# First tiles of three output projections begun inside the attention ahead of them

## The chip, the cores and the metric

The kernel runs on one core of one Trainium2 chip, in one launch. The metric is the device time of an execution in microseconds (us). Engines: TensorE (PE, with its weight loads PEld), VectorE (DVE), ScalarE (ACT), GpSimd (POOL) and SyncE (SP, which only issues transfers here). Lower is better.

## The reference

A decoder of two layers takes 1024 prompt tokens and 8 sample tokens (one per sequence of a batch of 8), width 1024, all in fp32. In words and cut to what matters:

```python
for l in range(2):
    hp = rms_norm(xp, norm_mix[l])
    # layer 0: short convolution beside banded attention; layer 1: pooling beside dilated attention
    mix = concat(conv_or_pool(hp), windowed_attention(hp))
    xp = xp + mix @ w_out
    mk, mv = rms_norm(mem, norm_mem[l]) @ w_ca_kv[l]
    q = rms_norm(xp, norm_ca[l]) @ w_ca_q[l]
    xp = xp + softmax(q @ mk.T / 16) @ mv @ w_ca_o[l]      # 4 heads of 256, 256 memory rows
    g, u = rms_norm(xp, norm_ffn[l]) @ w_ffn_in[l]
    xp = xp + (silu(g) * u) @ w_ffn_out[l]
y = rms_norm(xp, norm_final)
```

The same is done for the sample tokens, with their own caches, and new rows of the caches are outputs too. Layer 1's attention is dilated: three patterns of keys, combined by their softmax weights.

## The kernel before, in words

Activations lie transposed: partitions are features, a tensor `[128, 8, 1032]` is 8 chunks of 128 features by 1032 tokens. A linear map runs in units: one unit is one block of 128 output features, made of 8 chunks. The tokens are cut in three tiles of 344 columns, so a unit is 3 tiles x 8 chunks. To keep fp32's precision each operand is split in a high part (`*_hi`, type fp32r) and a low part (`*_lo`, the rest), and a chunk takes three matmuls: high x high, high x low and low x high. So one tile is 24 matmuls and one unit 72. They are issued by `passes` (line 712), called by `unit`.

Weights come by SP into `w_raw`, two slots; GpSimd makes their high part (line 563) and low part (line 567), half a unit at a time, into the slot of `w_hi` and `w_lo` that frees up; it may do so for the next unit once the present one has started (`unit_started`).

Attention writes its result into `mix1` (layer 1's pooling and dilated attention) or `mixc` (cross attention). Before the output projection that result is split too: `split` on ScalarE copies it into `h_hi` or `g_hi` (`copy`, line 1306), and `split` on VectorE subtracts into `h_lo` or `g_lo` (line 1906), in twelve pieces: three tiles by four groups of two chunks. Tensor for tensor:

- `out1` (from `linear_out`, 4 turns of 2 units) multiplies `h_hi`, `h_lo`; its results go to banks 0 to 2 of `linear`, and VectorE adds each into `x` (line 1924), squares are summed for the next norm (line 1876).
- `caout0` and `caout1` (from `ca_out`) do the same with `g_hi`, `g_lo`; here VectorE adds at line 2105, and beside this starts to make sums of `x` for the feed-forward part (`combine`, tiles named `c`).

What sets the order around this is written out by hand, engine by engine, with semaphores. Cross attention (`cross`) runs four heads. Each has units for queries and keys, then nine jobs: "S" scores (line 780), "T" turning the probabilities (line 816), "V" mixing the values (line 852), and at the end "R", the turning of the sample's result (line 823). Scores alternate between `ps_scores` and bank 0 of `linear`. In heads 0 to 2 the last steps are interleaved with the first key unit of the next head (`next_key`, line 956); in the last head `next_key` returns at once. The dilated attention of layer 1 runs in four pairs of heads; a pair's jobs ("S" line 1170, "T" line 1194, "V" lines 1224 and 1233) stand in the tables `DIL_KEY`, `DIL_FILL` and `DIL_DRAIN` between the tiles of the linear units. For the last pair there are none left, so its jobs follow each other. VectorE computes the maxima (line 2594), ScalarE the exponentials (line 1766) and the copies of turned blocks (line 1306, `pt`), VectorE the scaled results (lines 2632, 2634).

## Time and profile before

| | |
|---|---|
| median of 3 runs | 3014.34 us (3012.35 to 3015.76) |
| the profiled execution | 3013.3 us |
| its span, first to last instruction | 3011.5 us |
| mean granted TensorE clock | 0.986 |
| busy: PE, DVE, POOL, ACT | 96%, 55%, 45%, 26% |

The span is the time of the trace; the 1.8 us between it and the execution's own time lie around it. Starts in the rows are us from the span's start. The granted clock is a share of full speed, 2.4 GHz; 0.5 is 1.2 GHz. A matmul's row shows how long it took from start to finish; they overlap, so the pace is read from starts. In square brackets stands the idle time of the engine before a row, and what ended it.

### The profile page before, as it was taken

How to read it: one execution, taken by the hardware profiler on the slowest of the kernel's cores; microseconds unless marked ns; L12 is line 12 of the kernel's file. 1: busy time of each engine (PE TensorE's matmuls, PEld its weight loads, DVE VectorE, ACT ScalarE, POOL GpSimd, SP SyncE). 2: the span in 40 equal slices, each digit the busy share in tenths (PEclk: the TensorE clock that was granted, in tenths of full speed). 3: DMA queues.
4: the chain of work that ended last, by engine and by line, in shares of the span. 5: the costliest groups of instructions: out<-in, count | busy, mean ns of one | idle time of the engine just before them, and what ended most of it. 6: DMA issues, size and time to landing. Idle time of an engine off the chain costs nothing.

```text
span 3011.5 us, 58301 instructions
## 1 busy us (share of the span) xinstructions
PE 2877.5 (96%) x21217; PEld 2735.5 (91%) x21217; DVE 1642.7 (55%) x3290; ACT 796.9 (26%) x1832; POOL 1344.6 (45%) x1156
## 2 busy tenths in 40 slices
PE   7999999999899999999999999999997999999997
PEld 6888998989899999999887778988897999999996
DVE  5555642248755555655943336522368565565655
ACT  3333322132212221112323334212223111221112
POOL 2222343424665666655331102433336665565664
PEclk9999999999999999999999999999998999999998
DMA  3011133421111111111122221243210111111112
GB/s 129 29 35 35 52 122 113 151 74 35 43 48 49 49 50 49 54 42 56 60 71 78 78 71 64 85 145 121 106 42 30 55 56 42 56 42 56 54 44 71
DMA packets 52534, 198.83 MB, mean 66 GB/s; under 512 B 6961, under 2 KB 14001, under 8 KB 49081
## 3 DMA queue, kind: packets, MB, share of 16 engines
q1 hardware_dynamic: 36912, 130.51, 13.6%
q10 hardware_dynamic: 15504, 66.71, 6.2%
q8 instruction: 79, 1.29, 0.2%
q14 instruction: 39, 0.31, 0.0%
HBM read 184.34 MB, written 13.10 MB: 66 GB/s over the span
## 4 chain that ended last, share of the span: by engine, by line
PE 86%; DVE 7%; issue 3%; ACT 3%; POOL 1%; DMA 0%; ACTq 0%; DVEq 0%; POOLq 0%; SPq 0%
PE linear L712 46%; PE ps_scores L997 11%; PE ps_turned L997 8%; PE ps_mixed L997 4%; PE linear L997 4%; PE ps_mixed L852 2%; PE ps_turned L816 1%; PE ps_turned L1194 1%; PE ps_scores L780 1%; PE ps_mixed L1224 1%; PE ps_scores L1170 1%; DVE g_lo L1906 1%; POOL w_lo L567 1%; PE linear L780 1%; PE ps_mixed L848 1%
## 5 line engine op out<-in xcount | busy, mean ns | idle before, releaser
L567 POOL TENSOR_TENSOR w_lo<-w_raw,w_hi 128x512 fp32r<-128x512 f32 x492 | 687.7, 1407 | 259.1 <-ACT w_hi L1306 234.0
L563 POOL TENSOR_SCALAR w_hi<-w_raw 128x512 fp32r<-128x512 f32 x324 | 215.4, 678 | 1176.2 <-PE linear L712 993.1
L712 PE MATMUL linear<-h_hi,w_hi 128*128 128x344 f32 x1152 | 384.1, 333 | 27.9 <-POOL w_lo L567 13.3
L712 PE MATMUL linear<-h_lo,w_hi 128*128 128x344 f32 x1152 | 371.9, 323 | 0.0
L712 PE MATMUL linear<-h_hi,w_lo 128*128 128x344 f32 x1152 | 371.7, 323 | 0.0
L712 PE MATMUL linear<-hid_hi,w_hi 128*128 128x344 f32 x1056 | 339.1, 321 | 5.3 <-DVE x L2345 4.2
L712 PE MATMUL linear<-hid_hi,w_lo 128*128 128x344 f32 x1056 | 339.3, 321 | 0.0
L712 PE MATMUL linear<-hid_lo,w_hi 128*128 128x344 f32 x1056 | 338.9, 321 | 0.0
L2304 DVE TENSOR_TENSOR x<-linear,x 128x344 f32<-128x344 f32 x480 | 246.7, 514 | 144.4 <-PE linear L712 142.0
L997 PE MATMUL ps_scores<-c,w_hi 128*128 128x258 f32 x1584 | 304.6, 284 | 7.9 <-DVE c L2093 7.9
L712 PEld LDWEIGHTS linear<-h_hi,w_hi 128*128 128x128 f32 x1152 | 220.0, 191 | 45.6 <-issue 36.7
L712 PE MATMUL linear<-g_hi,w_hi 128*128 128x344 f32 x768 | 250.0, 326 | 5.8 <-DVE g_lo L1906 4.9
L997 PEld LDWEIGHTS ps_scores<-c,w_hi 128*128 128x128 f32 x1584 | 246.9, 190 | 8.6 <-DVE c L2093 8.3
L712 PE MATMUL linear<-g_hi,w_lo 128*128 128x344 f32 x768 | 246.6, 321 | 0.0
L712 PE MATMUL linear<-g_lo,w_hi 128*128 128x344 f32 x768 | 246.6, 321 | 0.0
L997 PE MATMUL ps_turned<-c,w_hi 128*128 128x258 f32 x1232 | 232.2, 285 | 10.9 <-ACT rs L1313 10.9
L1306 ACT ACTIVATE w_hi<-w_raw 128x512 fp32r<-128x512 f32 x168 | 100.8, 624 | 486.9 <-PE ps_mixed L997 295.8
L997 PE MATMUL ps_scores<-c,w_lo 128*128 128x258 f32 x792 | 225.3, 285 | 0.0
L567 POOL TENSOR_TENSOR w_lo<-w_sum,w_hi 128x512 fp32r<-128x512 f32 x132 | 178.2, 1350 | 96.2 <-ACT w_hi L1306 95.7
L712 PEld LDWEIGHTS linear<-h_lo,w_hi 128*128 128x128 f32 x1152 | 220.2, 191 | 0.5 <-issue 0.2
L712 PEld LDWEIGHTS linear<-h_hi,w_lo 128*128 128x128 f32 x1152 | 219.8, 191 | 0.0
L712 PEld LDWEIGHTS linear<-hid_hi,w_hi 128*128 128x128 f32 x1056 | 198.8, 188 | 6.5 <-DVE x L2345 5.0
(354 smaller groups left out, 6483.4 us busy)
## 6 DMA issues: line engine op xcount, KB each, us to landing
w_raw<-in_w SPq DMA_DIRECT2D x246, 512.0 KB, 3.5
kv_slotc<-in_mem_cache_k ACTq DMA_DIRECT2D x8, 2048.0 KB, 8.2
kv_slotc<-in_mem_cache_v ACTq DMA_DIRECT2D x8, 2048.0 KB, 10.2
kv_slot<-in_dil_k ACTq DMA_DIRECT2D x4, 1536.0 KB, 6.4
kv_slot<-in_dil_v ACTq DMA_DIRECT2D x4, 1536.0 KB, 6.6
out_y<-answer ACTq DMA_DIRECT2D x6, 688.0 KB, 6.7
x<-in_x ACTq DMA_DIRECT2D x2, 1376.0 KB, 10.2
out_dil_v_out<-v ACTq DMA_DIRECT2D x4, 516.0 KB, 3.6
```

Of the source, the lines that this page charges most:

```text
L563: pool.tensor_scalar(out, src, 1.0, 0.0, ALU.mult, ALU.add).then_inc(sem["hi_split"], 1)
L567: return pool.tensor_tensor(out, src, hi.bitcast(F32), ALU.subtract).then_inc(sem[event], 1)
L712: mm = pe.matmul(out, w[:, slot, cols], a, start=(k == 0 and j == 0), stop=(k == n - 1 and j == 2))
L780: mm = pe.matmul(sc[:, 0:MEM], q[:, c, P * job:P * job + P], k[:, c, :], start=(c == 0), stop=(c == 1))
L816: mm = pe.transpose(ps_t[:, o:o + P], p[job % RING[kind]][:, o:o + P], ident[:])
L848: mm = pe.matmul(o, w, a, start=(j < 4), stop=(j >= len(todo) - 4), skip_group_check=True)
L852: mm = pe.matmul(ps_o[:, P * c:P * c + P], vnat[:, m, P * c:P * c + P], pt[:, P * m:P * m + P], start=(m == 0), stop=(m == 1))
L997: mm = pe.matmul(lin[bank][:, 0:PART], w[:, b % 4 // 2, c], a, start=(b in OPENING and kp == 0 and j == 0), stop=(kp == CH // 2 - 1 and j ...
L1170: mm = pe.matmul(ps_s[:, 512 * h:512 * h + P * nb], q1[r:r + HEAD, P * qb:P * qb + P], k1[r:r + HEAD, P * kb:P * kb + P * nb], start=True, ...
L1194: mm = pe.transpose(ps_t[:, to:to + P], p1[i][k % 3][:, 512 * h + P * b:512 * h + P * b + P], ident[:])
L1306: return act.activation(out, in_, ACT.Copy, **kw)
L2304: dve.tensor_tensor(x[:, 4 * half + n, a:b], lin[tile_plan(ph)[p][0]][:, 0:TILE], x[:, 4 * half + n, a:b], ALU.add).then_inc(sem["freed_dv ...
```

## The change

Nine of the twelve pieces of the split are called `SOONER` (three tiles by the chunk groups 0 to 2, that is chunks 0 to 5), the other three `LATER` (chunks 6 and 7). In the last dilated pair, and in the last cross attention head of each layer, ScalarE and VectorE make the `SOONER` pieces between the attention's own instructions. A new function `begin` issues matmuls of the first unit's tiles there: in the dilated pair chunks 0 to 5 of all three tiles, two chunks after each of eight score jobs and two behind `DIL_DRAIN`'s first entry; in each last head chunks 0 to 5 of tile 0, in four places (2, 2, 1, 1 chunks). Behind the attention the `LATER` pieces are split and `unit` adds chunks 6 and 7 to the tiles begun. The loops over turns of these projections are written out on TensorE, `p1_late` lies at the end of `h_lo`, and layer 0's `out0` keeps its twelve pieces. Line numbers in the order rows are those of the file that they come from.

```diff
     raise KeyError(phase)
+SOONER = [(t, q) for t in range(3) for q in range(3)]
+LATER = [(t, 3) for t in range(3)]
@@ -238,7 +242,8 @@
...
-        return at("lo_ready", source, 0, 4 * t + k // 2 + 1) if k % 2 == 0 else None
+        pieces = [(t_, q) for t_ in range(3) for q in range(4)] if source == "split0" else SOONER + LATER
+        return at("lo_ready", source, 0, pieces.index((t, k // 2)) + 1) if k % 2 == 0 else None
@@ -437,7 +442,7 @@
...
-        p1_late = over_h(("p1_late", [P, 1024], F32))[0]
+        p1_late = over(("p1_late", [P, 1024], F32), start=h_place + 4 * TOK * (2 * CH - 1))[0]
@@ -714,7 +721,26 @@
...
+            def begin(phase, t, chunks, hi, lo, slot):
+                a, b = TILES[t]
+                ready = chunk_ready({"out1": "split1"}.get(phase, f"casplit{phase[-1]}"))
+                if chunks[0] == 0:
+                    pe.wait_ge(sem["half_split"], at("half_split", phase, 0, 1))
+                    pe.wait_ge(sem["freed_dve"], bank_wait(phase, 0, t)[1])
+                for k in chunks:
+                    if t == 0 and k == CH // 2:
+                        pe.wait_ge(sem["unit_split"], at("unit_split", phase, 0, 1))
+                    if ready(t, k) is not None:
+                        pe.wait_ge(sem["lo_ready"], ready(t, k))
+                    c = slice(P * k, P * k + P)
+                    for j, (w, x_) in enumerate(((w_hi, hi), (w_hi, lo), (w_lo, hi))):
+                        mm = pe.matmul(lin[t][:, 0:b - a], w[:, slot, c], x_[:, k, a:b], start=(k == 0 and j == 0), stop=False)
+                        if t == 0 and k == 0 and j == 0:
+                            mm.then_inc(sem["unit_started"], 1)
@@ -722,12 +748,13 @@
...
-                    pe.wait_ge(sem[name], value)
+                    if t not in begun:
+                        pe.wait_ge(sem[name], value)
...
+                           pause=pause and (lambda: pause(t)), begun=6 if t in begun else 0)
@@ -870,6 +897,13 @@
...
+                if phase == "out1":
+                    p = unit(phase, 0, 0, 0, TILES, hi, lo, chunk_ready(source), begun=(0, 1, 2))
+                    unit(phase, 0, 1, p, TILES, hi, lo)
+                    for i in range(1, 4):
+                        for u in range(2):
+                            unit(phase, i, u, 3 * u, TILES, hi, lo)
+                    return
@@ -879,11 +913,11 @@
...
                 ph, source = f"caout{l}", f"casplit{l}"
-                enter(ph)
-                with pe.Fori(0, 3) as i:
-                    p = 0
+                p = unit(ph, 0, 0, 0, TILES, g_hi, g_lo, chunk_ready(source), begun=(0,))
+                unit(ph, 0, 1, p, TILES, g_hi, g_lo)
+                for i in range(1, 3):
                     for u in range(2):
-                        p = unit(ph, i, u, p, TILES, g_hi, g_lo, chunk_ready(source) if u == 0 else None)
+                        unit(ph, i, u, 3 * u, TILES, g_hi, g_lo)
@@ -945,6 +979,9 @@
                     def next_key(part):
                         if h == CA_HEADS - 1:
+                            if part == 0:
+                                pe.wait_ge(sem["exped"], at("exped", ph, 0, order_s("mem", 6) + 1))
+                            begin(f"caout{l}", 0, ((0, 1), (2, 3), (4,), (5,))[part], g_hi, g_lo, 0)
@@ -1275,6 +1312,13 @@
                     for what, k in DIL_FILL.get(position, ()):
                         step(what, k)
+                        if i == PAIRS - 1 and what == "S" and k in range(4, 12):
+                            begin_out(k - 4)
+                def begin_out(n):
+                    t, q = SOONER[n]
+                    begin("out1", t, (2 * q, 2 * q + 1), h_hi, h_lo, 0)
@@ -1290,6 +1334,8 @@
                 last = step
             for position in range(5):
                 drain(position)
+                if position == 0:
+                    begin_out(8)
@@ -1335,16 +1381,19 @@
...
-            def split(phase, mix, before, hi):
+            def high_piece(mix, hi, t, q):
+                c, (a, b) = slice(2 * q, 2 * q + 2), TILES[t]
+                copy(hi[:, c, a:b], mix[:, c, a:b]).then_inc(sem["hi_ready"], 1)
+            def split(phase, mix, hi, pieces):
                 act.wait_ge(sem["mixed_out"], at("mixed_out", phase))
                 act.wait_ge(sem["freed_dve"], at("freed_dve", phase))
                 act.wait_ge(sem["tile_done"], at("tile_done", phase))
-                for t, (a, b) in enumerate(TILES):
-                    for q in range(4):
-                        c = slice(2 * q, 2 * q + 2)
-                        copy(hi[:, c, a:b], mix[:, c, a:b]).then_inc(sem["hi_ready"], 1)
+                for piece in pieces:
+                    high_piece(mix, hi, *piece)
@@ -1474,11 +1523,24 @@
...
+                        sooner(7)
+                    def sooner(n):
+                        if h == CA_HEADS - 1:
+                            past_waits()
+                            high_piece(mixc, g_hi, *SOONER[n])
+                    if h == CA_HEADS - 1:
+                        act.wait_ge(sem["tile_done"], at("tile_done", ph, 0, 7))
+                        for n in range(4):
+                            sooner(n)
                     attention(ph, 0, "mem", mixc, 2 * h, p_c, ptc, psc, drawnc[h], values=(kv_slotc[:, :], dram["mem_cache_v"][l, h]),
-                              ahead={("T", 0): values_turned, ("V", 4): values_stored}, redrawn=False)
+                              ahead={("T", 0): values_turned, ("V", 1): lambda: sooner(4), ("V", 2): lambda: sooner(5),
+                                     ("V", 3): lambda: sooner(6), ("V", 4): values_stored, ("V", 5): lambda: sooner(8)}, redrawn=False)
                 redraw(CA_HEADS - 1)
-                split(f"casplit{l}", mixc, ph, g_hi)
+                split(f"casplit{l}", mixc, g_hi, LATER)
@@ -1770,6 +1832,10 @@
...
+                    if i == PAIRS - 1 and what == "S" and k in range(1, 10):
+                        act.wait_ge(sem["tile_done"], at("tile_done", ph, 0, 6))
+                        high_piece(mix1, h_hi, *SOONER[k - 1])
                     if what == "S":
                         if SCORE_ORDER.index(k):
                             exponential(SCORE_ORDER[SCORE_ORDER.index(k) - 1])
@@ -1897,14 +1963,13 @@
...
+            def split(phase, mix, hi, lo, pieces, done=0):
+                for n, (t, q) in enumerate(pieces):
+                    c, (a, b) = slice(2 * q, 2 * q + 2), TILES[t]
+                    dve.wait_ge(sem["hi_ready"], at("hi_ready", phase, 0, done + n + 1))
+                    dve.tensor_tensor(lo[:, c, a:b], mix[:, c, a:b], hi[:, c, a:b].bitcast(F32), ALU.subtract
+                                      ).then_inc(sem["lo_ready"], 1)
@@ -2044,18 +2109,28 @@
...
+                    def sooner(n):
+                        past_waits()
+                        split(f"casplit{l}", mixc, g_hi, g_lo, SOONER[n:n + 1], n)
...
                     for done, job in zip(jobs, jobs[1:]):
                         if job == 2:
                             empty(ph, 0, 8, vc[h][:, 1, :], mem_rs[:], MEM)
                         bias_of(job)
                         normalise(done)
+                        if h == CA_HEADS - 1:
+                            sooner(jobs.index(done))
                     normalise(jobs[-1])
+                    if h == CA_HEADS - 1:
+                        sooner(8)
...
-                split(f"casplit{l}", mixc, g_hi, g_lo)
+                split(f"casplit{l}", mixc, g_hi, g_lo, LATER, 9)
@@ -2637,6 +2712,9 @@
                     if what == "S":
                         peaks(k)
+                        if i == PAIRS - 1 and k in range(2, 11):
+                            past_waits()
+                            split("split1", mix1, h_hi, h_lo, SOONER[k - 2:k - 1], k - 2)
```

TensorE, layer 0's last head, after the last score job (`kc`, `qc`). Before:

```order
L780 MATMUL ps_scores<-kc,qc 128x256 x2
L852 MATMUL ps_mixed<-ptc,vnatc 128x128 x4
L816 MATMUL ps_turned<-ident,pc_ring 128x128 x2
L852 MATMUL ps_mixed<-ptc,vnatc 128x128 x4
L816 MATMUL ps_turned<-ident,pc_ring 128x128 x2
L852 MATMUL ps_mixed<-ptc,vnatc 128x128 x4
L809 MATMUL ps_turned<-ident,psc 128x128 x2
```

and in the changed kernel:

```order
L807 MATMUL ps_scores<-kc,qc 128x256 x2
L879 MATMUL ps_mixed<-ptc,vnatc 128x128 x4
L843 MATMUL ps_turned<-ident,pc_ring 128x128 x2
L739 MATMUL linear<-g_hi,w_hi 128x344
L739 MATMUL linear<-g_lo,w_hi 128x344
L739 MATMUL linear<-g_hi,w_lo 128x344
L739 MATMUL linear<-g_hi,w_hi 128x344
L739 MATMUL linear<-g_lo,w_hi 128x344
L739 MATMUL linear<-g_hi,w_lo 128x344
L879 MATMUL ps_mixed<-ptc,vnatc 128x128 x4
L843 MATMUL ps_turned<-ident,pc_ring 128x128 x2
```

Six multiplies of `caout0`'s first tile stand between a turning and the mixing behind it.

VectorE, last dilated pair, from the end of job 2's maxima on (`p_late`; the ISA rows are the maxima with their masks). Before:

```order
L2594 ISA p_late,peak_104<-ps_scores,mask_102 128x512
L2594 ISA peak_104 128x1
L2594 ISA p_ring,peak_104<-ps_scores,mask_102,peak_104 128x384
L2594 ISA peak_104 128x1
L2594 ISA p_ring,peak_104<-ps_scores,mask_102,peak_104 128x384
L2594 ISA peak_104 128x1
L2605 TENSOR_SCALAR binv_106<-peak_104 128x2
L2622 TENSOR_TENSOR den_105<-den_105 128x2
L2625 RECIPROCAL binv_106<-den_105 128x2
```

and in the changed kernel:

```order
L2669 ISA p_late,peak_104<-ps_scores,mask_102 128x512
L2669 ISA peak_104 128x1
L1971 TENSOR_TENSOR h_lo<-mix_90,h_hi 128x2x344
L2669 ISA p_ring,peak_104<-ps_scores,mask_102,peak_104 128x384
L2669 ISA peak_104 128x1
L2669 ISA p_ring,peak_104<-ps_scores,mask_102,peak_104 128x384
L2669 ISA peak_104 128x1
L2680 TENSOR_SCALAR binv_106<-peak_104 128x2
L1971 TENSOR_TENSOR h_lo<-mix_90,h_hi 128x2x344
L2697 TENSOR_TENSOR den_105<-den_105 128x2
L2700 RECIPROCAL binv_106<-den_105 128x2
```

A low part stands behind each pair of maxima, and the sums and reciprocal (`den`, `binv`) on which the mixing waits have moved behind it.

ScalarE, start of the same pair. Before:

```order
L1827 DMA out_dil_k_out<-k_92 128x1032
L1766 ACTIVATE p_ring,den_105<-p_ring,binv_106 128x512 x4
L1306 ACTIVATE pt_98<-ps_turned 128x512 x2
L1766 ACTIVATE p_late,den_105<-p_late,binv_106 128x512 x2
L1306 ACTIVATE pt_98<-ps_turned 128x512 x2
```

and in the changed kernel:

```order
L1893 DMA out_dil_k_out<-k_92 128x1032
L1352 ACTIVATE h_hi<-mix_90 128x2x344
L1828 ACTIVATE p_ring,den_105<-p_ring,binv_106 128x512 x2
L1352 ACTIVATE h_hi<-mix_90 128x2x344
L1828 ACTIVATE p_ring,den_105<-p_ring,binv_106 128x512 x2
L1352 ACTIVATE pt_98<-ps_turned 128x512 x2
L1352 ACTIVATE h_hi<-mix_90 128x2x344
```

A high part stands ahead of each exponential; two of them have moved in front of the copy `pt`.

## Rows read from the trace of the kernel before

**Rows 1.** The page's part 1: engine, busy us, share, instructions.

```profile
PE 2877.5 (96%) x21217; PEld 2735.5 (91%) x21217; DVE 1642.7 (55%) x3290; ACT 796.9 (26%) x1832; POOL 1344.6 (45%) x1156
```

**Rows 2.** Chain of waits, 640 to 730 us: start, us, what ran.

```profile
641.48 12.53 DVE g_lo L1906 x12
...
656.57 64.45 PE linear L712 x408
```

**Rows 3.** Timeline, TensorE, layer 0's last head: start, us, operation, [idle before].

```profile
630.56 0.38 PE L816 MATMUL ps_turned<-ident,pc_ring 128*128 128x128 f32 x2
631.56 1.16 PE L852 MATMUL ps_mixed<-ptc,vnatc 128*128 128x128 f32 x8 [0.61 <-ACT ptc L1306]
...
639.66 0.60 PE L823 MATMUL ps_turned<-ident,drawn_last 128*128 128x128 f32 x4
642.50 0.40 PE L712 MATMUL linear<-g_hi,w_hi 128*128 128x344 f32 x1 [2.24 <-DVE g_lo L1906]
```

**Rows 4.** The same view, third head.

```profile
572.94 0.38 PE L816 MATMUL ps_turned<-ident,pc_ring 128*128 128x128 f32 x2
573.08 0.36 PE L956 MATMUL linear<-mem_hi,w_hi 128*128 128x256 f32 x1
...
573.94 1.16 PE L852 MATMUL ps_mixed<-ptc,vnatc 128*128 128x128 f32 x8
```

**Rows 5.** Windows: us, busy us (instructions) by engine, granted clock, DMA share, GB/s.

```profile
643.50:647.00 3.50, 3.50 (x15) 3.50 (x14) 3.50 (x4) 3.50 (x6) 3.50 (x3) 0.51 0.00 0
1836.68:1840.00 3.32, 3.32 (x12) 3.32 (x13) 3.32 (x4) 3.32 (x6) 2.49 (x3) 0.50 0.55 229
```

**Rows 6.** Low parts, line 1906, then high parts: count, ns min/median/max, first and last start.

```profile
L1906 DVE TENSOR_TENSOR g_lo<-mixc,g_hi x24: 862/868/1961, 641.5 to 2179.1; 128x688 fp32r<-128x688 f32 x24
...
L1306 ACT ACTIVATE g_hi<-mixc x24: 757/762/776, 640.7 to 2174.0; 128x688 fp32r<-128x688 f32 x24
```

**Rows 7.** Timeline, layer 0's last head: VectorE, then ScalarE.

```profile
625.84 0.42 DVE L1951 TENSOR_REDUCE peak<-ps_scores 128x1 f32<-128x256 f32 x1 [0.93 <-PE ps_scores L780]
...
627.84 0.42 DVE L1951 TENSOR_REDUCE peak<-linear 128x1 f32<-128x256 f32 x1 [0.93 <-PE linear L780]
...
624.85 0.38 ACT L1306 ACTIVATE mixc<-ps_mixed 128x256 f32<-128x256 f32 x1 [0.89 <-PE ps_mixed L852]
```

**Rows 8.** Timeline, GpSimd: layer 1's last head, then the start of `out1`.

```profile
2141.88 1.28 POOL L563 TENSOR_SCALAR w_hi<-w_raw 128x512 fp32r<-128x512 f32 x2 [3.47 <-PE linear L712]
2143.12 2.52 POOL L567 TENSOR_TENSOR w_lo<-w_raw,w_hi 128x512 fp32r<-128x512 f32 x2
...
1837.51 2.28 POOL L563 TENSOR_SCALAR w_hi<-w_raw 128x512 fp32r<-128x512 f32 x2 [57.41 <-PE linear L712]
```

**Rows 9.** Waits of TensorE, 1798 to 1828.5 us: us in total, times, longest.

```profile
PE ps_turned L1194 <- ACT pt L1306: 2.2, 5, 0.7
PE ps_scores L1170 <- DVE peak L2594: 1.4, 3, 0.7
```

**Rows 10.** Windows, the last dilated pair from its fourth job on.

```profile
1797.94:1828.82 30.88, 26.64 (x289) 18.04 (x288) 15.95 (x73) 21.43 (x60) 0.00 (x0) 1.00 0.16 53
```

**Rows 11.** Timeline, ScalarE, start of the last dilated pair.

```profile
1795.52 0.71 ACT L1766 ACTIVATE p_ring<-p_ring,binv 128x512 f32<-128x512 f32 x1
1796.14 0.19 ACT L1766 ACTIVATION_READ_ACCUMULATOR p_ring<-p_ring,binv 128x1 f32 x1
1796.23 1.06 ACT L1306 ACTIVATE pt<-ps_turned 128x512 f32<-128x512 f32 x2
```

**Rows 12.** Chain of waits at the start of `out1`, then TensorE's timeline there.

```profile
1836.68 13.35 PE linear L712 x69
...
1833.45 0.44 PE L1249 MATMUL ps_turned<-ident,drawn 128*128 128x128 f32 x2 [0.50 <-ACT drawn L1306]
1836.68 0.63 PE L712 MATMUL linear<-h_hi,w_hi 128*128 128x344 f32 x1 [2.80 <-DVE h_lo L1906]
```

**Rows 13.** Waits of VectorE, 656.57 to 721 us; then a window behind `caout`.

```profile
DVE x L2105 <- PE linear L712: 15.1, 12, 2.0
...
735.00:750.00 15.00, 9.94 (x60) 8.93 (x59) 14.72 (x17) 3.11 (x6) 11.38 (x9) 0.89 0.12 36
```

More of the change, by code:

```diff
@@ L697, in enter, with passes @@
                 pe.wait_ge(sem["freed_dve"], at("freed_dve", phase))
-            def passes(out, slot, terms, unit_first=False, ready=None, second_half=None, pause=None):
+            def passes(out, slot, terms, unit_first=False, ready=None, second_half=None, pause=None, begun=0):
                 n = len(terms)
                 for k, (cols, hi, lo) in enumerate(terms):
+                    if k < begun:
+                        continue
                     if pause and k == n // 2:
@@ L715, in passes, with unit @@
                 mm.then_inc(sem["tile_done"], 1)
-            def unit(phase, turn, u, p, tiles, hi, lo, ready=None, after=None, slot=None, pause=None):
+            def begin(phase, t, chunks, hi, lo, slot):
[14 more added lines that the diff above has]
+                            mm.then_inc(sem["unit_started"], 1)
+            def unit(phase, turn, u, p, tiles, hi, lo, ready=None, after=None, slot=None, pause=None, begun=()):
                 pe.wait_ge(sem["half_split"], at("half_split", phase, turn, u + 1))
@@ L729, in unit @@
                            second_half=at("unit_split", phase, turn, u + 1) if t == 0 else None,
-                           pause=pause and (lambda: pause(t)))
+                           pause=pause and (lambda: pause(t)), begun=6 if t in begun else 0)
                     if after:
@@ L1695, in out_and_memory @@
                 act.dma_start(mem_raw[:], dram["mem"]).then_inc(loads[f"mem{l}"], 16)
-                split(f"split{l}", mix, f"att{l}", h_hi)
+                split(f"split{l}", mix, h_hi, LATER if l else [(t, q) for t in range(3) for q in range(4)])
                 act.wait_ge(loads[f"mem{l}"], 16)
@@ L1898, in inverse @@
                     inverse_tile(name, t)
-            def split(phase, mix, hi, lo):
-                for t, (a, b) in enumerate(TILES):
-                    for q in range(4):
-                        c = slice(2 * q, 2 * q + 2)
-                        dve.wait_ge(sem["hi_ready"], at("hi_ready", phase, 0, 4 * t + q + 1))
-                        dve.tensor_tensor(lo[:, c, a:b], mix[:, c, a:b], hi[:, c, a:b].bitcast(F32), ALU.subtract
-                                          ).then_inc(sem["lo_ready"], 1)
+            def split(phase, mix, hi, lo, pieces, done=0):
[4 more added lines that the diff above has]
+                                      ).then_inc(sem["lo_ready"], 1)
             def empty(phase, turn, p, out, factor, w=TILE):
@@ L2489, in out_and_memory @@
                 dve.wait_ge(sem["mixed_out"], at("mixed_out", f"split{l}"))
-                split(f"split{l}", mix, h_hi, h_lo)
+                split(f"split{l}", mix, h_hi, h_lo, LATER if l else [(t, q) for t in range(3) for q in range(4)], 9 * l)
                 zero(ph)
```

## The prediction

> **What bounds the kernel now.** I read the page's busy shares first: the reader is to see TensorE busy for 96% of the span and nothing else near it [rows 1]. So a change gains only where it removes time in which TensorE has nothing to run, or runs slowly. The views to read next are the chain of waits and the timelines around the three joints that the diff touches: last head of cross attention to `caout` in layer 0 (near 642 us), the same in layer 1 (near 2168 us, with the same pattern), and last dilated pair to `out1` (near 1837 us). A multiply of 344 columns takes 0.158 us at full clock when they follow each other (64.45 us for 408) [rows 2].
>
> At the first joint the last turning of the attention ends at about 640.3, and `caout` starts at 642.50 after 2.24 us of idle, released by VectorE's first `g_lo` [rows 3]. VectorE then works without a break on twelve low parts (12.53 us from 641.48), and another 2.56 us pass until TensorE starts the second unit at 656.57 [rows 2]. So the first unit, 72 multiplies or 11.38 us of work, takes 14.07 us. Of the 2.7 us of excess the clock makes 1.7: from 643.5 to 647.0 it was granted 0.51, and 0.49 x 3.5 us is lost [rows 5]. The other 1.0 us is waiting for low parts and for the bank that VectorE empties late.
>
> At the dilated joint the idle stretch is 2.80 us, and then the clock is at the lower of its two levels, 1.2 GHz [rows 5, 12]. The first unit takes the 13.35 us of 69 multiplies plus 3 x 0.158, 13.82 us [rows 12].
>
> **The change at the two cross attention joints.** High and low parts of nine of the twelve pieces (a piece is two chunks by one tile) are made earlier, during the last head. 18 multiplies of tile 0 go to four places between the attention's last steps; behind it three pieces are made as before and 54 of the first unit's 72 multiplies remain. The wait is not removed: the last piece of tile 0 still goes copy, ScalarE high part, VectorE low part, so the 2.24 us stand [rows 3].
>
> From the first multiply behind the attention to the second unit's it will take 54 x 0.158 = 8.53 us plus the same 1.7 us of slow clock, 10.2 us in place of 14.07: 3.9 us less. VectorE is no limit there: it has three low parts in place of twelve, and the 2.56 us behind them [rows 2], so it is free after some 5 us where TensorE needs 10.
>
> What is added. The third head already carries six multiplies of 256 columns between these same steps, and its steps are as far apart as the last head's: 572.94 to 573.94 there, 630.56 to 631.56 here, both 1.00 us [rows 3, 4]. So they are hidden. Six of 344 columns are longer by 6 x 0.158 x 88 / 344 = 0.24 us, some 0.2 behind the pipeline's start; two of the places get six, the other two three, which fit: 0.4 us in all. ScalarE's pieces take 0.76 us [rows 6]; four go before the head's first exponential, five into idle stretches such as the 0.89 us before the row at 624.85 [rows 7]: nothing. Without that idle each would cost its 0.76. VectorE's pieces take 0.87 us where nothing disturbs them and up to 1.96 us beside GpSimd's splits of weights [rows 6]. VectorE idles 0.93 us in each job of 2.0 us [rows 7], so 0.87 fits by a hair. The early ones meet GpSimd's 2.5 us of low parts (at 2143.12 in layer 1 [rows 8]), and a multiply of attention waits for what stands behind them: I put 0.5 us, between nothing and the 1.09 us by which a disturbed piece is longer. Sum for one joint: 3.9 - 0.4 - 0.5 = 3.0 us; both 6.0 us.
>
> Two edits cost nothing. The loops over turns are written out: the 64.45 us of multiplies [rows 2] run over three turns' ends without a gap, so the loop cost nothing either. `p1_late` moves from the start of `h_hi` to the last chunk of `h_lo`, which no early piece writes.
>
> Is the gain kept? From 735 us VectorE is busy 14.72 of 15 us and TensorE waits for it [rows 13]: a place where a gain could end. But up to 721 VectorE itself waited 15.1 us in twelve places for TensorE's tiles [rows 13], so its load begins when the tiles come, and moves with them. I keep all of it.
>
> **The change at the dilated joint.** Here all nine early pieces get their multiplies inside the pair: 54, or 8.53 us, in nine groups of 0.95 us; 18 close the first unit. Behind the attention stand 8.53 us less, with the wait of 2.80 us and the slow clock unchanged, because the last three pieces are still begun behind the attention's last copy. The price is the pair's own length. From its fourth job on TensorE waits only 2.2 + 1.4 = 3.6 us [rows 9]; if the groups filled all of it, the pair would be 8.53 - 3.6 = 4.9 us longer. That is the lower bound. To it I add one high part of 0.76 us [rows 6] that lands where ScalarE has no idle at all, before the copy at 1796.23, which follows its exponentials at once [rows 11]; and one disturbed low part. GpSimd splits the next unit's weights as soon as the first group starts, so this moves from 1837.51 [rows 8] into the pair, and 1.96 - 0.87 = 1.1 us [rows 6] goes on VectorE. 4.9 + 0.8 + 1.1 = 6.8 us longer, a gain of 8.53 - 6.8 = 1.7 us. The upper bound is everything on the path: 8.5 of TensorE, 9 x 0.76 = 6.8 of ScalarE and 9 x 0.87 = 7.8 of VectorE, 23.1 us longer. I stay near the lower one since ScalarE is busy 21.4 and VectorE 16.0 of 30.9 us [rows 10]: both have room, though ScalarE comes to 28.2.
>
> The trace has low parts of 0.87 us and of 1.96 us [rows 6], and GpSimd's high parts took 2.28 us beside them, 1.28 otherwise [rows 8]. The Trainium skill, "SBUF — State Buffer", section "Who interferes with whom", says that a VectorE instruction with two SBUF inputs and a GpSimd one that reads SBUF take a port pair as an exclusive lock, and that the second blocks until the first is done. By that rule all four GpSimd instructions that move, 1.28 + 2.52 = 3.8 us undisturbed [rows 8], could hold up VectorE inside the pair; it would be 4.9 + 0.8 + 3.8 = 9.5 us longer and this joint a loss of 1.0. That speaks against the change, on the side of the third rival below.
>
> **Sum.** 6.0 + 1.7 = 7.7 us. The profiled execution took 3013.3 us, span 3011.5 and 1.8 around it; less 7.7 that is 3005.6. It lies 1.0 us under the median of the runs (3014.34), so I predict 3006.6 us. A measurement can tell about 0.2%, 6.0 us, from no change: below 3008.3 is faster, above 3020.4 slower.
>
> **Rivals.** First, the clock holds. With the attention's idle places filled, TensorE is not granted the lower level at these joints, and the losses go: 1.7 + 1.7 and, at the dilated joint, 13.82 - 11.38 = 2.4 us, together 5.8: 3000.8. For it: more is fed before each joint. Against it: the idle stretches of 2.24 and 2.80 us remain, and the clock was low behind both kinds [rows 5, 12]. The Trainium skill, "TensorE: Matmul & The Clock Gate", section "What's actually happening", says that activity releases the throttle and that idle is the throttled state. The low clock behind the gaps agrees, and by that rule a fuller attention could keep it up. Chance 0.14.
>
> Second, the gain at the cross joints is not kept: VectorE's full stretch from 735 us does not move, and only the dilated 1.7 us stay: 3012.6. The 15.1 us of waits speak against it. Chance 0.08.
>
> Third, the dilated pair gives a loss: its steps form one chain through three engines, each of which gets pieces, and it becomes 10.5 us longer, 2.0 more than it gives: 6.0 - 2.0 = 4.0 gained, 3010.3. ScalarE's 28.2 of 30.9 us speaks for it, the idle of VectorE against [rows 10]. Chance 0.16.
>
> Fourth, slower: in the same chain nearly every piece stands in series, 23.1 us longer, 14.6 more than the 8.5 given; less the 6.0 that is 8.6 us slower: 3022.9. From 14.5 us of lengthening on, the kernel is slower than before. Against it: ScalarE idles 9.5 and VectorE 14.9 us of those 30.9 [rows 10], and pieces have nothing to wait for when an engine idles. Chance 0.03.
>
> The forecast has 0.59; its own range, 3003 to 3009.5, comes from 2.4 to 3.9 us for each cross joint and 0 to 3.6 at the dilated one. Some 0.12 of it lies beyond 3008.3. Faster: 0.47 + 0.14 and 0.03 of the third rival where it is milder, 0.64; slower 0.03; same 0.33. The range of 8 in 10 is 3000.5 to 3012.5.
>
> **What would show it.** In the profile after: the idle before the first multiply behind each attention still 2.2 and 2.8 us; from it to the second unit about 10 us at the cross joints, with no wait for VectorE's sums; the dilated pair 6 to 8 us longer from its second score job to the last turning, with hardly any wait for ScalarE; low parts of 0.87 us there but for one to four long ones; GpSimd's split of the second unit inside the attention. Wrong would be: a pair 10 us longer (third rival), full clock behind the joints (first), or TensorE waiting 3 us longer for VectorE after 735 us (second).

## The result and the profile after

The changed kernel takes 2997.15 us (median of 5 runs, 2994.33 to 2997.83) where the kernel before takes 3014.34 (3012.35 to 3018.01 in 5 runs): ratio 0.9941, 95% interval 0.9928 to 0.9955. It is faster by 17.2 us, or 0.6%, where 7.7 us were forecast and the far end of the range was 13.8. The profiled execution took 2994.33, its span 2992.5.

The page's part 1, beside [rows 1]:

```profile
PE 2870.5 (96%) x21217; PEld 2729.6 (91%) x21217; DVE 1638.3 (55%) x3290; ACT 795.9 (27%) x1832; POOL 1338.4 (45%) x1156
```

The instructions are the same in number, and TensorE is busy for 7.0 us less; this row does not tell why. The other 12 us of the 19.0 by which the span is shorter are idle time that went.

The chain at layer 0's joint, then at layer 1's, beside [rows 2]:

```profile
641.20 0.89 DVE g_lo L1971
642.23 74.45 PE linear L719 x462
...
2155.78 72.91 PE linear L719 x462
```

VectorE has one low part on the chain in place of twelve, and TensorE runs through. Less the 64.45 us of the 408 behind it, the 54 multiplies of the first unit take 10.0 us in layer 0 and 8.5 in layer 1, in place of 14.07. Two windows tell these apart (us, busy us by engine, granted clock):

```profile
642.80:646.10 3.30, 3.30 (x13) 3.30 (x13) 3.01 (x6) 0.00 (x0) 0.00 (x0) 0.50 0.00 0
...
2156.00:2164.00 8.00, 8.00 (x52) 8.00 (x52) 4.87 (x9) 0.99 (x3) 0.00 (x0) 1.00 0.01 2
```

TensorE in the last head of layer 0, beside [rows 3]:

```profile
630.17 0.38 PE L843 MATMUL ps_turned<-ident,pc_ring 128*128 128x128 f32 x2
630.31 0.41 PE L739 MATMUL linear<-g_hi,w_hi 128*128 128x344 f32 x1
...
631.34 1.05 PE L879 MATMUL ps_mixed<-ptc,vnatc 128*128 128x128 f32 x8
...
639.39 0.60 PE L850 MATMUL ps_turned<-ident,drawn_last 128*128 128x128 f32 x4
642.23 0.39 PE L719 MATMUL linear<-g_hi,w_hi 128*128 128x344 f32 x1 [2.24 <-DVE g_lo L1971]
```

The six multiplies fit (1.17 us from turning to mixing, 1.00 before), and the 2.24 us of idle stand. Low parts, beside [rows 6], and then GpSimd's split of `out1`'s second unit, now inside the pair, beside [rows 8]:

```profile
L1971 DVE TENSOR_TENSOR h_lo<-mix,h_hi x24: 859/875/1966, 308.9 to 1833.2; 128x688 fp32r<-128x688 f32 x24
L1971 DVE TENSOR_TENSOR g_lo<-mixc,g_hi x24: 865/868/1955, 614.4 to 2156.3; 128x688 fp32r<-128x688 f32 x24
```

```profile
1791.22 1.20 POOL L568 TENSOR_SCALAR w_hi<-w_raw 128x512 fp32r<-128x512 f32 x2 [21.33 <-PE linear L739]
1792.39 3.13 POOL L572 TENSOR_TENSOR w_lo<-w_raw,w_hi 128x512 fp32r<-128x512 f32 x2
```

The longest low part in the pair took 1.05 us. TensorE's waits, 1785 to 1827 us, beside [rows 9]:

```profile
PE ps_mixed L1248 <- ACT pt L1352: 0.8, 1, 0.8
PE ps_mixed L1261 <- DVE mix L2709: 0.7, 1, 0.7
PE ps_turned L1231 <- ACT pt L1352: 0.2, 1, 0.2
```

Only the last row lies in the stretch that [rows 9] covers (1788.5 to 1824.4 us here): 3.6 us in the kernel before, 0.2 now. The other two stand behind it in both kernels, with 0.72 and 0.79 us.

Windows of the pair from the same multiply to the same multiply as in [rows 10], and of the joint behind it, beside [rows 5]:

```profile
1788.51:1824.77 36.26, 35.35 (x344) 26.78 (x343) 22.75 (x81) 25.32 (x66) 4.30 (x4) 1.00 0.18 60
...
1834.10:1837.30 3.20, 3.20 (x13) 3.20 (x12) 2.21 (x5) 0.96 (x2) 0.00 (x0) 0.50 0.09 36
```

From its fourth job on the pair is 5.4 us longer (36.26 against 30.88). TensorE's first multiply behind it and the chain from there, beside [rows 12]: the 2.80 us of idle stand here too, and the stretch at the low clock is 3.4 us long where it was 6.8.

```profile
1832.64 0.40 PE L719 MATMUL linear<-h_hi,w_hi 128*128 128x344 f32 x1 [2.80 <-DVE h_lo L1971]
```

```profile
1832.64 83.95 PE linear L719 x522
```

**A ledger of the two traces.** All of VectorE's instructions but the low parts come in the same order in every kernel here, so any two traces can be laid side by side at them. In each stretch between the same two instructions, the changed kernel's time less that of the kernel before is: layer 0's last head and joint -3.5 us (0.5 longer, then 4.0 shorter); last dilated pair +6.15, its joint -9.2, so -3.1; layer 1's head and joint -5.0. Together 11.6. The other 7.4 us lie in stretches whose instructions are the same: the first 47 us -0.8, layer 0's feed-forward turns -1.9, the norms from 1440 to 1530 us -3.8, the start of layer 1's feed-forward part -1.3, the end +0.5, all else -0.1. So there were two questions: why the joints give more than 7.7, and whether the 7.4 is chance.

### The profile page after: what moved, and what is told of

It reads as the page before. It is cut to its first block, busy times and chain, and to the rows that moved or that the text cites. A ratio compares the mean times of both kernels' runs of the same rounds, so it can differ in the third digit from the quotient of the medians.

```text
span 2992.5 us, 58217 instructions
## 1 busy us (share of the span) xinstructions
PE 2870.5 (96%) x21217; PEld 2729.6 (91%) x21217; DVE 1638.3 (55%) x3290; ACT 795.9 (27%) x1832; POOL 1338.4 (45%) x1156
## 4 chain that ended last, share of the span: by engine, by line
PE 89%; DVE 6%; issue 2%; ACT 2%; POOL 0%; DMA 0%; ACTq 0%; DVEq 0%; POOLq 0%; SPq 0%
PE linear L719 47%; PE ps_scores L1034 12%; PE ps_turned L1034 8%; PE ps_mixed L1034 4%; PE linear L1034 4%; PE ps_mixed L879 2%; PE ps_turned L843 1%; PE ps_turned L1231 1%; PE ps_scores L1207 1%; PE ps_mixed L1261 1%; PE ps_scores L807 1%; PE linear L807 1%; PE ps_mixed L875 1%; PE ps_mixed L887 1%; PE linear L993 1%
## 5 line engine op out<-in xcount | busy, mean ns | idle before, releaser
L568 POOL TENSOR_SCALAR w_hi<-w_raw 128x512 fp32r<-128x512 f32 x324 | 209.1, 658 | 1164.0 <-PE linear L719 937.6
L719 PE MATMUL linear<-h_hi,w_hi 128*128 128x344 f32 x1134 | 376.4, 332 | 27.5 <-POOL w_lo L572 13.1
L719 PE MATMUL linear<-h_lo,w_hi 128*128 128x344 f32 x1134 | 364.8, 322 | 0.0
L719 PE MATMUL linear<-h_hi,w_lo 128*128 128x344 f32 x1134 | 364.7, 322 | 0.0
```

Source lines behind the costliest of these rows:

```text
L568: pool.tensor_scalar(out, src, 1.0, 0.0, ALU.mult, ALU.add).then_inc(sem["hi_split"], 1)
L719: mm = pe.matmul(out, w[:, slot, cols], a, start=(k == 0 and j == 0), stop=(k == n - 1 and j == 2))
```

## The experiments

"Joints" is, in that kernel's one trace, layer 0's, the dilated and layer 1's stretch against the kernel before; medians are of 5 to 11 runs. The runs were made on several chips, and each ratio is to runs of the kernel before on the same chip, so ratios compare better than medians do.

| kernel | median us | ratio to before (95%) | joints, us |
|---|---|---|---|
| before_again | 3013.11 | 0.9996 (0.9987 to 1.0005) | 0.0, +0.1, 0.0 |
| cross0_only | 3007.82 | 0.9982 (0.9973 to 0.9991) | -3.5, 0, 0 |
| cross1_only | 3006.23 | 0.9974 (0.9963 to 0.9985) | 0, 0, -3.5 |
| dilated_only | 3009.71 | 0.9985 (0.9976 to 0.9994) | 0, -3.2, 0 |
| after_again | 2993.75 | 0.9936 (0.9923 to 0.9950) | -5.0, -3.1, -5.0 |
| no_begin | 3001.41 | 0.9960 (0.9946 to 0.9974) | -4.8, -0.7, -4.8 |
| fill_cross | 2990.35 | 0.9924 (0.9911 to 0.9938) | -7.5, -1.9, -7.5 |
| fill_all | 2989.41 | 0.9917 (0.9904 to 0.9931) | -7.5, -3.3, -7.5 |
| unrolled_only | 3010.26 | 0.9992 (0.9983 to 1.0001) | +0.1, +0.1, 0.0 |
| no_begin_unrolled | 2996.53 | 0.9941 (0.9928 to 0.9955) | -4.8, -2.7, -4.8 |
| low_after_sums | 2990.23 | 0.9917 (0.9903 to 0.9930) | -7.5, -3.6, -7.5 |
| out0_unrolled | 3012.22 | 0.9992 (0.9983 to 1.0002) | 0, 0, 0 |
| fill_all_out0 | 2990.10 | 0.9920 (0.9906 to 0.9933) | -7.5, -4.1, -7.5 |
| after_looped | 3003.87 | 0.9964 (0.9950 to 0.9978) | -3.5, -1.0, -5.0 |

**before_again** is the kernel before, unedited.

> The kernel before, once more. Theory B (the two traces differ by 7.6 us in stretches that the diff does not touch, and that part is what an execution happens to get): its median lies within 2 us of the kernel before, but its profile, laid beside the first one, differs by some us in such stretches: other places with the clock at 0.5, other ones of the 0.6 us waits for w_lo in the feed-forward turns. Theory A (each kernel has its own fixed pattern and the difference in those stretches belongs to the edit): the same places of low clock (643, 746, 760, 777, 1442, 1487, 1835, 2169 us) and the same three waits of 0.6 us, offsets within 0.3 us throughout.

Theory B held in part: the same code gave 1.6 us more in this trace than in the first. The clock was low at nearly the same places, as Theory A had it, and at one more near the end; but other feed-forward turns were long. Each of the 18 takes either 63.2 or 63.9 us; the first trace had four long ones, this one seven. The long ones hold a wait like this (TensorE, kernel before):

```profile
934.09 0.38 PE L997 MATMUL ps_mixed<-c,w_hi 128*128 128x258 f32 x1 [0.27 <-POOL w_lo L567]
```

**One joint at a time.** cross0_only, cross1_only and dilated_only keep the change at one joint and leave the others as before (`AHEAD` names the splits made early, `OPENED` the projections begun early and written out):

```diff
+AHEAD = ("casplit0",)
+OPENED = ("caout0",)
...
-                        if h == CA_HEADS - 1:
+                        if h == CA_HEADS - 1 and f"casplit{l}" in AHEAD:
```

> Only layer 0's cross attention joint is changed. Both traces side by side give this joint 3.3 us. Theory B: 3.3 us less than before (between 2 and 5), whatever the stretches behind it do. Theory A (an earlier arrival also changes what comes behind it, the norms at 1440 to 1520 us and the feed-forward turns): 3.3 + 1.9 + 3.8, about 9 us less.

> Only layer 1's cross attention joint is changed. Forecast for this joint was 3.0 us; the traces give 5.0, of which 1.7 is the clock that did not fall. Theory B: 3.3 us less than before (2 to 5). Theory A (the clock's hold and the 1.3 us at 2286 us belong to the edit): 6.3 us less.

> Only the dilated joint is changed. Forecast 1.7 us less; the traces give 3.1 us: the pair 6.2 us longer, and 9.3 less behind it. Theory B: 3.1 us less than before (1.5 to 4), pair longer by 6.2. Theory A: 3 us too, since nothing behind it moved by more. If the three single changes add up to about 9.5 to 11 us while all together measured 17.2, the changes are not additive and the rest is the interplay or the clock; if they add up to 17, the joints were under-estimated by the traces' comparison.

The ratios sum to 17.7 us and the joints in the traces to 10.2. The three are additive, then, but each gives more than its joint shows, which neither theory had foreseen. Each also writes out its own projection's loop, to which the last group of runs returns. dilated_only also settled a term of the prediction. In it layer 0's joint is as before, but the clock did not fall. The window of [rows 5], TensorE's first multiply and the chain of [rows 2], in this trace:

```profile
643.50:647.00 3.50, 2.88 (x17) 2.38 (x16) 3.50 (x3) 3.50 (x6) 3.50 (x3) 1.00 0.00 0
```

```profile
640.85 0.40 PE L722 MATMUL linear<-g_hi,w_hi 128*128 128x344 f32 x1 [2.24 <-DVE g_lo L1983]
```

```profile
639.83 12.54 DVE g_lo L1983 x12
654.92 5.13 PE linear L722 x31
```

From 640.85 to 654.92 are 14.07 us, to the hundredth what it took with the slow clock. VectorE set that pace: its twelve low parts, and 2.5 us of its work behind them until the bank for the second unit is free. TensorE, at full clock, only waited more for the low parts (1.3 us once it had begun, where the kernel before has 0.2). The slow stretch cost nothing there before; layer 1's joint, without it, is of the same length too.

**after_again** is the changed kernel, unedited.

> The changed kernel, once more. The three single changes took off 5.4, 7.8 and 4.5 us by their ratios, 17.7 together, while their traces show the joints 3.5, 3.5 and 3.2 us shorter. Theory B (the rest is what an execution happens to get in stretches that the diff does not touch): the profile shows more of the feed-forward turns of 63.9 us than the one of 18 that the first profile had, and other values at 1440 to 1520 us; the joints as before: cross attention 3.5 us shorter than in the kernel before (5.0 where the clock holds), dilated 3.2. Theory A (the edit also changes the unchanged stretches): again at most two long turns of 18. The median stays 15 to 18 us under the kernel before.

It has four long turns out of 18, as the first trace of before has, but its untouched stretches are again 6.3 us under that trace. Chance alone was getting unlikely. Both cross joints give 5.0 us, with the clock full in both.

**no_begin** has `OPENED = ()` and `AHEAD` with all three:

> High and low parts early as in the changed kernel at all three joints, but no multiply of the projections is begun in the attention: all 72 stand behind it. Theory V (in the kernel before the first unit of a cross joint is paced by VectorE's twelve low parts, 14.1 us whether the clock is low or not): a cross joint's first unit takes 72 x 0.158 = 11.4 us at full clock, 13.1 with one low stretch, so 1.0 to 2.7 us less, minus some 0.3 for the disturbed early low parts; 1 to 2.4 us gained at each. At the dilated joint TensorE's slow clock paced the first unit: nothing gained behind, and the pair longer by what ScalarE's and VectorE's pieces cost alone; between 1 and 3 us of the 6.15. Theory C (the prediction's: the clock made 1.7 of the 2.7 us of excess): 0.5 to 1 us gained at a cross joint. Sum by V about 0 to 3 us less than before, by C 1 us more to 1 us less.

Both theories were far off, and this is the best lesson of the series: 12.7 us less than before by medians. TensorE at the start of its `caout0`:

```profile
640.42 0.60 PE L855 MATMUL ps_turned<-ident,drawn_last 128*128 128x128 f32 x4
640.78 0.40 PE L722 MATMUL linear<-g_hi,w_hi 128*128 128x344 f32 x1
```

No idle stretch. Chunks 0 to 5 of tile 0 are 18 multiplies, 2.84 us, and their parts are ready, so they run in the 2.24 us in which chunks 6 and 7 are still being made. I had let the wait stand since the last piece is no earlier; but TensorE is idle only if nothing else is ready. The change puts those 18 into the attention and then waits idle for the last piece. By the traces, beginning them early brings it 0.3 us at a cross joint at full clock (5.0 in after_again against 4.8), and where the clock falls it is behind (3.5). At the dilated joint it is much the same: with the loops written out (no_begin_unrolled, below) and at full clock the early parts alone give 2.7 of the 3.1 us.

**fill_cross, fill_all** give TensorE work for these waits:

```diff
+                begin(ph, 1, range(6), g_hi, g_lo, 0)
-                p = unit(ph, 0, 0, 0, TILES, g_hi, g_lo, chunk_ready(source), begun=(0,))
+                p = unit(ph, 0, 0, 0, TILES, g_hi, g_lo, chunk_ready(source), begun=(0, 1))
```

and fill_all also has

```diff
-                        if i == PAIRS - 1 and what == "S" and k in range(4, 12):
+                        if i == PAIRS - 1 and what == "S" and k in range(4, 10):
...
-                if position == 0:
-                    begin_out(8)
+            for n in (6, 7, 8):
+                begin_out(n)
```

> The changed kernel, and at each cross joint chunks 0 to 5 of tile 1 (18 multiplies, 2.84 us) are multiplied before tile 0 is closed, so in the 2.24 us in which TensorE waited for the last low part of tile 0. Theory I (the wait is only order): each joint 2.2 us shorter than in the changed kernel, 4.5 in all, about 2992.5 us. If the idle stretch is also what lets the clock fall there, up to 1.7 more per joint where it would have been low. Rival: VectorE's adds of tiles 0 and 1 and the squares on ScalarE move late together and cost it again: less than 1 us gained.

> The same, and at the dilated joint the last three of nine groups (18 multiplies) stand behind the attention's last step, not inside the pair. Theory I: the 2.80 us of waiting are filled by them, and the pair, 6.15 us longer than before for nine groups, becomes shorter by about a third of it, 2.0 us; behind it nothing is added, since 2.84 us fit the wait. 2.0 us less than fill_cross, about 2990.5. With the clock held at that joint 1.7 less. Rival: the groups were hidden inside the pair and the pair's length comes from ScalarE's and VectorE's pieces: then nothing is gained, within 0.5 us of fill_cross.

```profile
638.52 0.60 PE L850 MATMUL ps_turned<-ident,drawn_last 128*128 128x128 f32 x4
638.88 0.40 PE L739 MATMUL linear<-g_hi,w_hi 128*128 128x344 f32 x1
```

The rows are of layer 0's cross joint in fill_cross: no idle time either. Each cross joint is 2.5 us shorter than in after_again. fill_all is the fastest kernel by its median, though fill_all_out0, low_after_sums and fill_cross cannot be told from it. In all three traces with its dilated joint (fill_all, fill_all_out0, low_after_sums) the clock fell at the pair's start. Against after_again that had cost 1.4 to 2.2 us by the point at 1804 us of the kernel before. So at full clock, by estimate, fill_all's pair is some 4.8 us longer than before, as Theory I had it, and its joint would give 2.4 us more than after_again's. No trace shows this pair at full clock.

**low_after_sums** moves VectorE's early low parts in the pair behind `den` and `binv`:

```diff
-                            past_waits()
-                            split("split1", mix1, h_hi, h_lo, SOONER[k - 2:k - 1], k - 2)
+                            held.append(k - 2)
...
+                    if what in "TV" and held:
+                        n = held.pop()
+                        past_waits()
+                        split("split1", mix1, h_hi, h_lo, SOONER[n:n + 1], n)
```

> fill_all, with VectorE's early low parts in the dilated pair moved behind the sum and reciprocal (den, binv) that they delayed by 0.85 us in six places. Theory P (the pair's length comes from these, since the mixing waits for binv): the pair 2 to 3 us shorter than in fill_all at the same clock, that is 2.5 to 3 us longer than in the kernel before instead of some 4.8 (fill_all's 6.9 held a low stretch of the clock of 6.8 us); about 2986.5 us. Rival: the pair is paced by TensorE and ScalarE, and VectorE's pieces stood in idle time: within 0.5 us of fill_all.

The pair is 0.3 us shorter where Theory P had 2 to 3, and the ratio is the same. VectorE's pieces stood in idle time.

**Loops.** unrolled_only writes out the turns and makes nothing early (`p1_late` lies where the change puts it, as in all runs with `AHEAD`); no_begin_unrolled does it to no_begin; out0_unrolled to a loop that the change leaves alone; fill_all_out0 adds that to fill_all; after_looped puts the changed kernel's later turns back:

```diff
-                with pe.Fori(0, 3) as i:
-                    p = 0
-                    for u in range(2):
-                        p = unit(ph, i, u, p, TILES, g_hi, g_lo, chunk_ready(source) if u == 0 else None)
+                p = unit(ph, 0, 0, 0, TILES, g_hi, g_lo, chunk_ready(source))
+                unit(ph, 0, 1, p, TILES, g_hi, g_lo)
+                for i in range(1, 3):
+                    for u in range(2):
+                        unit(ph, i, u, 3 * u, TILES, g_hi, g_lo)
```

is unrolled_only's edit in `ca_out`, with its like for `out1`; after_looped's there is

```diff
-                for i in range(1, 3):
+                with pe.Fori(1, 3) as i:
```

> The kernel before, its turns of caout0, caout1 and out1 written out on TensorE as in the changed kernel, and nothing made early. Open point: by the traces the three joints of the changed kernel are 12 to 13 us shorter (at full clock), while its runs are 17 to 20 us under those of before; 5 us or so stand in stretches whose instructions are the same. Theory L (the written-out loops change these stretches, through the program's instructions or its start): 3 to 6 us less than before, the joints unchanged to 0.1 us. Theory N (the loops cost nothing, as the prediction had it): within 1.5 us of before.

> no_begin, with the same loops written out. It stood at 3001.4 us, with its cross joints 4.8 us shorter than before, since TensorE began the unit at once (the 2.24 us of waiting were gone) and never waited for VectorE again. Theory L: 3 to 5 us less than no_begin, 2997. Theory N: within 1.5 us of it.

> The kernel before with the four turns of out0, a loop that the change leaves alone, written out on TensorE; 7002 instruction rows there in place of 6583, as many as in dilated_only. Theory S (it is the program's size or place that counts, not what runs at a joint: the load of x on ScalarE's queue landed after 10.2 to 10.5 us in three kernels with all loops, 9.1 to 9.9 with one written out, 8.8 to 9.2 with all three): x lands after about 9.2 us, and the first 47 us are 0.5 to 1.5 shorter than in before. The median 1 to 3 us less than before. Theory R (the written-out loops save where they run): x lands after 10.2 to 10.5 as before; the median within 1 us, or less by what out0's own stretch shows.

> fill_all, the fastest so far, with out0's turns written out too. By theory S another 0 to 1.5 us off fill_all's 2989.4; by theory R the same as fill_all. Its profile also gives fill_all's dilated pair once more: 4.8 us longer than before if the clock is full in it (theory I), 6.9 if the clock is low at 1781 us again or if the pair's length has nothing to do with the clock.

> The changed kernel with the later turns of caout0, caout1 and out1 put back into loops on TensorE; only each first turn is written out. 7015 rows on TensorE in place of 7552 (before: 6583), close to dilated_only and out0_unrolled. All early work stands. By what the joints show it should keep their 10 to 13 us. Theory S (the size of TensorE's program): x lands after about 9.2 us as in those two, the first 47 us are 0.5 us longer than in the changed kernel, and the median is 1 to 2.5 us above its 2993.8 to 2997.2: about 2997.5. Theory R (written-out turns save where they run): 3 us above, 2998.5 to 3000, with the joints' own stretches longer in the trace. If it stands at 2995.5, the changed kernel's mean, the loops had no part in its time beyond the start.

By medians the written-out loops are worth 3.3 us in unrolled_only, 4.9 in no_begin_unrolled against no_begin, and after_looped stands 6.7 us over the changed kernel's 2997.15, with its joints' work kept (2 us of it are a low stretch of the clock in its traced pair). None of the three is clear of noise alone: the first's interval reaches 1.0001, and those of the other pairs overlap by 0.0009 and 0.0005. By means, each against before on its own chip and after_looped against both sets of the changed kernel's runs, they are 2.6, 4.8 and 8.0 us; each weighted by the scatter of its runs, they come to 4.0 us together, standard error 0.7 (an estimate). out0's gave 2.9 by medians, an interval that reaches 1.0002, and nothing on top of fill_all. The prices differ more than I can explain. The joints' own stretches did not move in unrolled_only, so it is not where these loops run. One place shows it in each trace, ahead of any loop: the load of `x` on ScalarE's queue (kernel before, then unrolled_only; the last number is us from issue to landing):

```profile
x<-in_x ACTq DMA_DIRECT2D x2, 1376.0 KB, 10.2
```

```profile
x<-in_x ACTq DMA_DIRECT2D x2, 1376.0 KB, 8.9
```

It took 10.2 to 10.5 us in the three kernels with TensorE's program of 6583 rows (instructions as written, a loop's body once), 9.0 to 9.9 in the five of 6858 to 7015, 8.8 to 9.2 in the eight of 7552 or more. Over the stretches that no edit touches and in which traces differ, the eight traces with all three loops written out sum to 1611.3 us (1609.1 to 1615.6), the eight others to 1615.5 (1612.6 to 1617.8): 4.3 less, standard error 1.0, in portions of 0.5 to 0.9 at the start, in the turns, the norms and the end. This grouping was made after the fact. What ties it to the program's size is open: place in memory and fetching of instructions both remain.

## Why the prediction was wrong

The direction, the place and most of the mechanism were right; the sum was 9.5 us too small. Step by step:

- "From the first multiply behind the attention to the second unit's it will take ... 10.2 us in place of 14.07": right with a low stretch (74.45 - 64.45 = 10.0), and 8.5 without.
- **The step that failed first** is "Of the 2.7 us of excess the clock makes 1.7". dilated_only had none of the slow clock and the same 14.07 us. VectorE paced the unit, so the slow clock only filled time in which TensorE would have waited, and I carried it over as a constant. Once VectorE is out of the way the clock is worth 1.5 us. That it holds at a joint is the first rival's event (chance 0.14). Of the eight traced cross joints changed like this it fell at four.
- Added cost at a cross joint, 0.4 + 0.5: measured 0.5 in all. The disturbed low parts (1.95 us, two in each last head) cost nothing. With this a cross joint gives 3.5 or 5.0 us, forecast 3.0.
- Dilated joint: pair 6.15 longer (forecast 6.8), 9.2 less behind it (forecast 8.5; the low clock lasted half as long). 3.1 in place of 1.7. Of the forecast's terms the filling of TensorE's waits came out (5.4 us from the fourth job on, 4.9 at least by the sum) and so did ScalarE's high part (0.7 us ahead of it in after_again, 0.8 by the sum); the disturbed low part took 0.2 us more, not 1.1. The third rival is out: in that stretch TensorE waits 0.2 us for ScalarE and never for VectorE. GpSimd's four instructions took 1.20 and 3.13 us there, and VectorE lost 0.2 us to them, not 3.8. The rule of the Trainium skill, "SBUF — State Buffer", section "Who interferes with whom", agrees with the trace; it was my 3.8 that did not follow from it. By it the second instruction waits for what is left of the first. The low part of 1.05 us began 0.3 us before GpSimd's high part ended, and GpSimd's next low part took 1.89 us in place of 1.26. The low part of 1.95 us in the last head began 0.1 us behind a GpSimd low part of 1.3 us.
- "The 2.24 us stand": true of this kernel, but argued from the wrong end. It stands because TensorE has nothing else begun; no_begin and fill_cross show it gone.
- **The step that failed most** is "the loop cost nothing either". It looked for gaps at the turns' ends, where there are none. unrolled_only, no_begin_unrolled and after_looped put 3 to 7 us on it by medians, some 4 together, all elsewhere. How the loops come to cost this stays open.
- Second rival (gain given back from 735 us on): out; the stretch from 719 to 800 us is +0.2 us.

Sum: joints 10.1 (clock low in both cross joints) to 13.2 us, loops 3 to 7, against 17.2. What an execution happens to get (long turns, norms between 86.1 and 90.1 us by where low stretches fall) moved the untouched stretches by up to 6.5 us between traces of two kernels with the same loops. Two traces of one kernel are nearer, 1.6 us apart for before and 1.1 for the changed kernel, but 29 runs of before on one chip spread from 3006.99 to 3018.49. Of the 7.4 us found in the first comparison about 4 belong to the loops and 3 to chance: an estimate from the two groups of eight, and no run rules out that each kernel has a share of its own in the 3.

## What to carry to other kernels

When two engines both explain a slow stretch, removing one does not give back its own share: find which of them is last at each point, in a trace in which the other is absent. Before moving work ahead of a wait, ask whether making its inputs early already lets it run inside the wait. And compare several traces at the same instructions before crediting a difference between two: single pairs here disagreed by up to 6.5 us in code that was the same in both.

## What the runs showed of the hardware

The clock fell behind the 2.24 us of idle at 10 of 12 unchanged cross joints and 4 of 8 changed ones, and at none of the 12 where that idle was filled (no_begin, no_begin_unrolled, fill_cross, fill_all, low_after_sums and fill_all_out0). But for the one at each trace's end, low stretches were 3.4 or 6.8 us long. Where they came was not fixed by the instructions: with the same ones up to there, the norms' stretch held 10.2 us of low clock in the kernel before and none in dilated_only, 3.8 us apart. And with a longer program for TensorE a load at the very start landed sooner, in 8.8 to 9.2 us in place of 10.2 to 10.5, for a reason that no run shows. Where one of VectorE's low parts and a GpSimd instruction on the weights met, the one that began second took longer by nearly what was left of the first (0.87 to 1.95 us, 1.26 to 1.89).
